# Nine places instead of six for split weight chunks, and another order of VectorE at the stage seams

## The reference, cut to what matters

```python
f1:    x = x + 0.5 * swiglu(rmsnorm(x), w_gate, w_up, w_down)      # 1024 -> 2816 -> 1024
mixer: h = rmsnorm(x); proj = h @ w_in                             # v, u, q, k, v, two gates
       y_a = spatial_gating(gelu(u), layernorm(gelu(v)), w_s)      # 4 groups, blocks of 128 rows
       y_b = stick_breaking_attention(q, k, v)                     # 16 heads of 64
       x = x + (g_a * (y_a @ w_a) + g_b * (y_b @ w_b)) @ w_out
f2:    x = rmsnorm(x + 0.5 * swiglu(rmsnorm(x), ...))
gla:   x = layer_norm(ALPHA * x + gla_mixer(x))                    # gated linear attention
f3:    x = layer_norm(ALPHA * x + swiglu_ffn(x))
moba:  x = layer_norm(ALPHA * x + moba_mixer(x))                   # 8 heads of 128
f4:    x = layer_norm(ALPHA * x + swiglu_ffn(x))
```

## Time and profile before

| what | us |
|---|---|
| median of 3 runs | 1271.23 (1270.84 to 1273.45) |
| profiled execution, its time | 1272.64 |
| its span in the profile | 1270.9 |
| PE busy | 1249.0 |
| DVE busy | 759.8 |
| ACT busy | 604.5 |
| PE's waits for `wl` in all | 3.8, in 7 places |
| mean granted clock of PE, of full speed | 0.997 |

### The profile page before, as it was taken

How to read it: one execution, slowest core, us unless ns; L and a number is a source line. 1 busy time by engine, 2 the same in 40 slices (tenths; PEclk the granted TensorE clock), 3 DMA queues, 4 the chain that set the end, 5 groups by cost and what they waited for, 6 DMA issues and landing times.

```text
span 1270.9 us, 15256 instructions
## 1 busy us (share of the span) xinstructions
PE 1249.0 (98%) x5959; PEld 1019.3 (80%) x5959; DVE 759.8 (60%) x1027; ACT 604.5 (48%) x784; POOL 43.2 (3%) x99
## 2 busy tenths in 40 slices
PE   8999999999999999999999999999999999999997
PEld 6888887887778888888877657888887887888886
DVE  6755546756676665555456557555557767655554
ACT  7444435556657454444345434344434554444441
POOL 2000002100000000000000010000000000000000
PEclk9999999999999999999999999999999999999999
DMA  8655555655545466565565345655564644655551
GB/s 290 194 192 190 195 165 168 243 176 149 144 153 185 153 200 209 183 196 185 168 161 164 108 128 198 213 188 185 191 197 153 197 140 125 240 190 167 193 186 52
DMA packets 119831, 226.03 MB, mean 178 GB/s; under 512 B 8120, under 2 KB 16320, under 8 KB 119760
## 3 DMA queue, kind: packets, MB, share of 16 engines
q1 hardware_dynamic: 117184, 216.10, 52.7%
q0 software_dynamic: 2560, 8.95, 2.4%
q10 hardware_dynamic: 16, 0.00, 0.0%
HBM read 223.98 MB, written 1.05 MB: 177 GB/s over the span
## 4 chain that ended last, share of the span: by engine, by line
PE 92%; DVE 5%; issue 1%; POOL 1%; ACT 1%; DMA 0%; SPq 0%; DVEq 0%; POOLq 0%; ACTq 0%
PE ps L430 28%; PE ps L435 28%; PE ps L440 28%; PE ps L378 3%; DVE wl L1467 1%; DVE X L1557 1%; DVE X L1563 1%; PE ps L759 1%; PE ps L761 1%; PE ps L590 1%; PE ps L603 1%; DVE st L1548 0%; DVE XTL L1505 0%; DVE X L1568 0%; DMA raw<-in_ff_w_gate_dram 0%
## 5 line engine op out<-in xcount | busy, mean ns | idle before, releaser
L1467 DVE TENSOR_TENSOR wl<-raw,wh 128x1024 fp32r<-128x1024 f32 x405 | 482.9, 1219 | 246.3 <-ACT wh L909 243.7
L909 ACT ACTIVATE wh<-raw 128x1024 fp32r<-128x1024 f32 x405 | 418.9, 1055 | 226.5 <-PE ps L440 202.6
L430 PE MATMUL ps<-wh,XTH 128*128 128x512 f32 (+1 forms) x1184 | 453.7, 387 | 0.0
L435 PE MATMUL ps<-wl,XTH 128*128 128x512 f32 (+1 forms) x1184 | 446.0, 380 | 3.8 <-DVE wl L1467 3.8
L440 PE MATMUL ps<-wh,XTL 128*128 128x512 f32 (+1 forms) x1184 | 348.1, 380 | 0.4 <-DVE XTL L1513 0.2
L435 PEld LDWEIGHTS ps<-wl,XTH 128*128 128x128 f32 x1184 | 223.5, 189 | 46.8 <-DVE wl L1467 6.1
L430 PEld LDWEIGHTS ps<-wh,XTH 128*128 128x128 f32 x1184 | 223.7, 189 | 45.6 <-issue 4.7
L440 PEld LDWEIGHTS ps<-wh,XTL 128*128 128x128 f32 x1184 | 216.1, 189 | 44.7 <-DVE XTL L1505 1.3
L430 PE MATMUL ps<-wh,HHf 128*128 128x512 f32 x352 | 137.8, 391 | 0.0
L435 PE MATMUL ps<-wl,HHf 128*128 128x512 f32 x352 | 137.1, 390 | 0.0
L440 PE MATMUL ps<-wh,HLf 128*128 128x512 f32 x352 | 108.4, 389 | 0.0
(11 more groups left out here) (279 smaller groups left out, 939.9 us busy)
## 6 DMA issues: line engine op xcount, KB each, us to landing
raw<-in_ffn_w_gu_dram SPq DMA_DIRECT2D x88, 512.0 KB, 4.5
raw<-in_w_in_dram SPq DMA_DIRECT2D x56, 512.0 KB, 3.7
raw<-in_ff_w_up_dram SPq DMA_DIRECT2D x44, 512.0 KB, 4.7
raw<-in_ff_w_down_dram SPq DMA_DIRECT2D x44, 512.0 KB, 4.0
raw<-in_ffn_w_down_dram SPq DMA_DIRECT2D x44, 512.0 KB, 4.3
raw<-in_ff_w_gate_dram SPq DMA_DIRECT2D x40, 512.0 KB, 4.0
raw<-in_gla_w_in_dram SPq DMA_DIRECT2D x24, 512.0 KB, 4.4
raw<-in_moba_w_in_dram SPq DMA_DIRECT2D x24, 512.0 KB, 4.4
```

What stands on the lines that cost most here:

```text
L430: e.matmul(o, lh[:, kt, rows(t)], wh[:, s, w], start=kt == 0, stop=False)
L435: e.matmul(o, lh[:, kt, rows(t)], wl[:, s, w], start=False, stop=False)
L909: e.activation(wh[:, j % NS, 0:m], raw[:, j % NR, 0:m], ACT.Copy).then_inc(S("wh"), 1)
L1467: e.tensor_tensor(wl[:, j % NS, 0:m], raw[:, j % NR, 0:m], wh[:, j % NS, 0:m].bitcast(F32), ALU.subtract).then_inc(S("wl"), 1)
```

## The change

There are three more places for the high and three for the low parts (`wh2`, `wl2`, MORE = 3). Their memory is taken at the bottom of the room that the stages share. From block q0 to the first chunk of wb1, and from gv0 to the first chunk of go0, the stages themselves need that room, and chunks then have only the first six places (`held`). A planner gives each chunk the place whose last use is the longest ago, and ACT waits for that use (`freed[j]`), which is chunk j-9 where all nine places are open, and j-6 in the held stretches. `reach(n)` is the last chunk that can be split once chunk n is used.

```diff
-                    if j >= NS:
-                        e.wait_ge(S("used"), j - NS + 1)
+                    if freed[j] >= 0:
+                        e.wait_ge(S("used"), freed[j] + 1)
...
+        held = [(first_chunk("q0"), first_chunk("wb1")), (first_chunk("gv0"), first_chunk("go0"))]
+        place, freed = [], []
+        last_use = [-NS - MORE + i for i in range(NS + MORE)]
+        for j in range(len(chunks)):
+            for begin, end in held:
+                if j == begin:
+                    last_use[NS:] = [end] * MORE
+            i = min(range(NS + MORE), key=lambda i: (last_use[i], i))
+            place.append(i)
+            freed.append(last_use[i])
+            last_use[i] = j
...
+        def reach(n):
+            j = max(n + 1, 0)
+            while j < len(chunks) and freed[j] <= n:
+                j += 1
+            return j - 1
+
+        def lead(n):
+            return min(reach(n), n + NS)
+
+        OPENING, CLOSING = ("f1g0", "vg0", "f2g0", "gq", "f3g0", "mq0", "f4g0"), ("f1d1", "wo1", "f2d1", "go1", "f3d1",
+                                                                                  "mo1", "f4d1")
```

In the programs of ACT and of DVE the number of the last chunk to split comes from `lead`, which gives the same chunk as before (j+4 at step j). Only in the closing blocks, ahead of the t=0 pass, is it `reach`, up to three chunks more. DVE's part is this (ACT's has `end + 1` in place of `end - 1` and keeps its loop to `end - 2`):

```diff
                 if tail:
-                    low_to(end - tail - 1 + LEAD)
+                    ahead = (reach if name in CLOSING else lead)(end - tail - 2)
+                    low_to(min(ahead, end - 1) if name in OPENING else ahead)
                     yield 0
-                    for j in range(end - tail, end - 2):
-                        low_to(j + LEAD)
+                    for j in range(end - tail, end - tail + 1 if name in CLOSING else end - 2):
+                        low_to(lead(j - 1))
                     at_chunk["step"] = end - 1
                     yield 1
```

More of the change, by code:

```diff
@@ L18 @@
 NS = 6
-LEAD = NS - 1
+MORE = 3
 HALVES = 4
@@ L102, in build @@
         with ExitStack() as phase:
+            wh2, wl2 = [sb(n, [P, MORE, 1024], FR, phase) for n in ("wh2", "wl2")]
             rot = [sb(f"rot{i}", [P, 2, 16], F32, phase) for i in range(8)]
@@ L417, in pe_products @@
             b, at, end, width, kts = blocks[name]
-            s, (_, n, _, k0) = j % NS, chunks[j]
+            _, n, _, k0 = chunks[j]
+            high, low = wh_of(j), wl_of(j)
             o = ps[:, bank_of(name, t), 0:width]
@@ L429, in pe_products @@
                     wait(e, "h", t, kt)
-                e.matmul(o, lh[:, kt, rows(t)], wh[:, s, w], start=kt == 0, stop=False)
+                e.matmul(o, lh[:, kt, rows(t)], high[:, w], start=kt == 0, stop=False)
                 if t == 0 and j < HALVES:
@@ L434, in pe_products @@
                     e.wait_ge(S("wl"), j + 1)
-                e.matmul(o, lh[:, kt, rows(t)], wl[:, s, w], start=False, stop=False)
+                e.matmul(o, lh[:, kt, rows(t)], low[:, w], start=False, stop=False)
             for c in range(n):
@@ L439, in pe_products @@
                     wait(e, "l", t, kt)
-                ins = e.matmul(o, ll[:, kt, rows(t)], wh[:, s, w], start=False, stop=kt == kts - 1)
+                ins = e.matmul(o, ll[:, kt, rows(t)], high[:, w], start=False, stop=kt == kts - 1)
             if t == 1:
@@ L926, in block @@
                 if tail:
-                    high_to(end - tail - 1 + LEAD)
+                    ahead = (reach if name in CLOSING else lead)(end - tail - 2)
+                    high_to(min(ahead, end + 1) if name in OPENING else ahead)
                     yield 0
                     for j in range(end - tail, end - 2):
-                        high_to(j + LEAD)
+                        high_to(lead(j - 1))
                     at_chunk["step"] = end - 1
@@ L1222, in gla @@
                         copy_first("gq", QG, cols(0))
-                high_to(blocks["low"][1] - 1 + LEAD)
+                high_to(lead(blocks["low"][1] - 2))
                 def split_o(half):
@@ L1420, in high_half @@
                 e.wait_ge(S(f"raw{j}" if h else f"raw{j}first"), 16)
-                e.activation(wh[:, j % NS, cols(h)], raw[:, j, cols(h)], ACT.Copy).then_inc(S("wh" if h else "wh_first"), 1)
+                e.activation(wh_of(j)[:, cols(h)], raw[:, j, cols(h)], ACT.Copy).then_inc(S("wh" if h else "wh_first"), 1)
             key = ("x", 1, 0, 0)
```

51 lines of the change are left out of this document (31 added, 20 removed).

## The result

| what | before | after |
|---|---|---|
| median, us | 1271.24 (19 runs, 1270.01 to 1274.21) | 1274.72 (19 runs, 1273.06 to 1276.65) |
| ratio after / before | | 1.0024 (95%: 1.0017 to 1.0030) |
| profiled execution / its span, us | 1272.64 / 1270.9 | 1275.03 / 1273.3 |
| PE's waits for `wl`, us and times | 3.8 in 7 | 5.5 in 4 |

The kernel became 3 us slower (3.5 by the medians, 3.0 by the ratio). The forecast was 1268.6 us, 2.6 faster. The two profiled executions are 2.4 us apart, so a ledger between their traces explains most of it.

What follows compares the result with a forecast made beforehand. TensorE is busy for 1249.0 of 1270.9 us, so only its waits can be won. Seam gains of -4.7, vg1 +1.6 and start +0.5 make -2.6 us: from 1271.23 to 1268.6 us, range 1266.3 to 1271.3.

Steps and rivals of the forecast that it cites:

- Three seams behind a d1 block: Splits moved into VectorE's idle time before the first readout gain 1.6 us at f3d1, 0.9 at f2d1, 0 at f1d1.
- Three closings: Seams behind 4-chunk closing blocks: earlier splits gain 0.3 us at go1, 1.45 at mo1, 0.45 at wo1.
- the 1.6 us wait in go1: Three more splits make go1's t=0 readout and norm 1.6 us late, and TensorE waits that long before its transposes.
- half of the gain: Rival: seam gains 2.5 us in place of 4.7, giving 1270.8 us; chance 0.10.
- the ten splits run out of loads: Rival "slower": splits ahead of a d1 block's first readout lack loads, +5.8 us, 1277 us; chance 0.08.
- The start: In f1g0 the fifth chunk's split comes 3.1 us later, delaying GpSimd and ScalarE; loss 0.5 us, ends 0 and 1.5.
- the stated end of 1.5: Upper end given for the loss at the start (f1g0), where 0.5 us was taken.
- vg1: vg1's first chunk, split behind the norm of VG, makes TensorE wait one chunk earlier; loss 1.6 us.
- The ends of 1.1 and 2.7: Range of the vg1 loss: 2.7 us if U lands as before, 1.1 if it lands 1.6 earlier.
- The costly mixer: Rival: U lands as before, costing 2.7 us in vg1, and the slow clock lasts longer; 1270.3 us, chance 0.19.
- The clock was set equal: Slow stretch behind the vg1 wait expected again, change 0; ends: gain 1.5 us or loss 1.2 us.
- a constant 1.41 us: Distance of before's median below its profiled execution, used to go from 1270.0 us profiled to the forecast 1268.6.

Runs made afterwards that it cites:

- e4: Changed kernel with the three opening moves (f1g0, vg0, gq) taken back, all else as changed: 1266.29 us, ratio to before 0.9963.
- e1: Changed kernel with one move taken back: in f1g0 the fifth chunk is split ahead of the XTL again: 1271.06 us, ratio to before 0.9996.
- e7: e4 with GpSimd loading U ahead of the two norm gains instead of behind them: 1267.25 us, ratio to before 0.9967.
- e2: Changed kernel with one move taken back: vg1's first chunk is split ahead of the norm of VG again: 1269.32 us, ratio 0.9985.
- e6: Kernel before, with its six places, plus only the three split moves in f1g0, vg0 and gq: 1278.55 us, ratio to before 1.0052.
- e3: Changed kernel with one move taken back: in gq the small chunk is split ahead of XTL again: 1273.12 us, ratio to before 1.0012.
- e5: Changed kernel with nine places and planner kept, but all splits in the order of before: 1271.62 us, ratio to before 1.0001.
- e9: e4 with the closing blocks filled less deep and U still loaded third: 1265.95 us, ratio to before 0.9940.

## Why the prediction was wrong

**The gains were right.** Three seams behind a d1 block: 2.5 predicted (1.6, 0.9, 0), 2.44 measured. Three closings: 2.2 predicted, 2.26 measured, with the 1.6 us wait in go1 in its place. e4 shows them without the losses. Neither "half of the gain" nor "the ten splits run out of loads" came. The losses, not the gains, carried the time out of the range.

**The start is the first step that failed** ("PE wants that chunk at 24.30. Loss 0.5 us"). The delay of each link was right to 0.2 us: 3.1 for GpSimd, 2.7 for ScalarE, 23.6 for the split. At TensorE's next need 0.88 was paid. But the working ended at this first consumer. VectorE's row has no idle time from there to the readout of HB, so the remaining delay was not absorbed: 1.47 us more, 2.35 in all, outside the stated end of 1.5. e1 took the move back and both waits went.

**vg1 was mis-sized.** 1.6 was predicted, from a relief of U by 1.1 us, of the 1.6 that 0.524 MB could give at most; 2.25 was measured, since the relief was 0.46 us. The ends of 1.1 and 2.7 held it. The Trainium skill ("DMA: Bandwidth & Descriptors", section Queues, rings and completion order) says that each DMA engine goes round between its queues, and the prediction read a loss of 1.1 out of it. The trace doesn't agree with that use of the rule. The load that went was not the only neighbour: the two gains, of 512 KB each, run beside U from GpSimd's own queue. With U first (e7) the wait only moved to them. The costly mixer, which had 0.19, was the nearer case there.

**The clock was set equal, and in the runs it was not.** In the two profiled executions the stretch in vg1 is the same. But the prediction expected a wait of 3 to 5 us in place of 2 and put the change of the clock at nothing in its main sum. The mean clock over the runs is lower in all four kernels with the long wait in vg1, and taking the move back in e2 gave 5.0 us by the ratios where its waits account for 2.2. The prediction had this as an end, at up to 1.2 us; the estimate from the mean clocks is up to 2.3.

**gla was not looked at, and its cost stays open.** The text ahead of the prediction puts nearly all of TensorE's waits into the six seams. Of the 14 us in before's list of waits 5.4 lie there, 2.07 in vg1, 2.9 at the start and the rest inside the stages. The prediction read the openings only at f1g0 and vg0, although the rule `min(ahead, end - 1)` moves a split in gq too. The ledger has 0.70 us there at `lowT`, 0.17 at `LA` and the 1.59 of the slow stretch. But the three other kernels with the same move have no wait for `lowT`, so the 0.70 belong to one execution and no run shows that the move causes them. The slow stretch stands in three of the four kernels with the move (after, e2, e6, not e1) and in none of the seven without it. That speaks for a link, but no row shows one, each is a single execution, and the runs of e2, with the move in them, have a mean clock of 0.9980, like those of before. It may be what made e3 1.5 us faster than after; this stays open.

**The median.** The working went from before's profiled execution to its median by a constant 1.41 us. That execution, at a mean clock of 0.997, has the slow stretch in vg1, and after's profiled one lies only 0.31 above its median. Of the 6.1 us between forecast and median, 1.1 is this difference (1.41 - 0.31), 1.85 the start, 0.65 vg1 and 2.5 gla; the gains add nothing. The 1.1 and the 2.5 rest on the two executions that happened to be profiled, so this division holds for them and not for the runs as a whole.

## What to carry to other kernels

When an instruction on an in-order engine becomes late by d, follow that engine's row until the first idle time that covers d, and price every consumer on the way; the first one is not the last. A rule applied to a whole class of places must be read at each of them in the order. Take a new wait in one trace for the cost of an edit only when the other kernels with the same edit show it too: the wait for `lowT` stood in one of four. Put work that can be early ahead of a cross-engine wait, but only so much as the idle time in front of it holds: in go1 three splits more met 1.76 us of idle and ran 1.6 us over, and taking two of them away was worth 0.9 us net.

## What the hardware showed that was not expected

- A stretch at the 1.2 GHz level of 3 to 4 us costs 1.6 us in gla. In vg1's profiled executions it follows waits of 2.07 (before), 2.12 (e2), 2.2 (e5) and 3.9 to 4.4 us (after, e1, e3, e6), and does not follow waits of 1.68 (e4), 2.21 (e7) and 2.76 us (e9). In gla it comes in after, e2 and e6 with no wait over 0.7 us ahead of it in the 15 us before, and not in e1, whose waits there are no longer. Several runs of one kernel differ by it. The kernels with the longest wait in vg1 have the lowest mean clock over their runs, but what decides in one execution stays open. For a change of 0.2% it means that terms don't add up between profiled executions, as in e2, whose edit is worth 2.2 us by its waits and 5.0 by the ratios.
- Loads issued by GpSimd within 2 us of each other move each other: with U third the landings are 4.4, 6.1 and 8.1 us (gain, gain, U, before), with U first 3.6 for it and 8.2 and 9.4 for the gains (e7). Beside two weight loads of 512 KB, U landed in 8.1 us in before and e2, 8.2 in e5 and 7.7 in e4; beside one, in 7.6 in after, 7.3 in e1, 7.2 in e3, 7.7 in e6 and 8.1 in e9. So the one load is worth some 0.5 us, and one execution scatters by as much.
- The load of 512 KB that `lowT` waits for in gla took 10.3 us (e7) to 13.0 us (after) from issue to landing, beside GpSimd's loads. The kernels without the move in gq have 10.3 to 12.5, those with it 11.9 to 13.0. A wait of 0.7 us on such a load is within this scatter.
